# First mixer of a two-layer hybrid backbone: the product of probabilities and values as unsplit fp32 matmuls of 64 output rows each, and the place of the spread of the softmax denominators

## The reference

```python
def softmax_with_sink(s, sink):
    s_all = jnp.concatenate([s, jnp.broadcast_to(sink, s.shape[:-1] + (1,))], axis=-1)
    return jax.nn.softmax(s_all, axis=-1)[..., :-1]

def attend(q, k, v, ok, sink, scale):
    s = jnp.einsum('bqhgd,bkhd->bhgqk', q, k).astype(jnp.float32) * scale
    if ok is not None:
        s = jnp.where(ok, s, NEG_INF)
    p = softmax_with_sink(s, sink[None, :, :, None, None])
    return jnp.einsum('bhgqk,bkhd->bqhgd', p.astype(v.dtype), v)

# latent queries see a window of latent keys and all context keys; context queries see context keys
bx = conformer_conv(px[..., i_u:], w_dw, b_dw, ln_g, ln_b)   # GLU, 31 taps, layer norm, SiLU
ox = jnp.concatenate([ax, bx], axis=-1) @ w_out
```

## Time and profile before

| | |
|---|---|
| median of 3 runs | 1679.69 us |
| profiled execution | 1684.07 us, its span 1682.2 us |
| PE busy | 1649.3 us, 98% |
| DVE busy | 1132.4 us, 67% |
| ACT busy | 603.7 us, 36% |
| POOL busy | 126.2 us, 8% |
| first mixer's attention loop | from 446 us to 573 us of the span |

### The profile page before, as it was taken

The page is one execution under the profiler, slowest core; times in us unless marked ns, Lnnn a source line. Parts: engine busy times, 40 slices in busy tenths (PEclk is TensorE's granted clock), DMA queues, the critical chain, the costliest instruction groups (busy, mean ns, idle before and its releaser), DMA issues.

```text
span 1682.2 us, 23652 instructions
## 1 busy us (share of the span) xinstructions
PE 1649.3 (98%) x8871; PEld 1414.0 (84%) x8871; DVE 1132.4 (67%) x1885; ACT 603.7 (36%) x817; POOL 126.2 (8%) x81
## 2 busy tenths in 40 slices
PE   8999999999999899999999999999999999999998
PEld 6788888889877698888888898888888888989997
DVE  5878777777585678787787873463333687666665
ACT  3321222223776532212212342212222356444443
POOL 0000000000796100000000000000000011000000
PEclk7999999999999999999999999999999999999999
DMA  7754554542211035555555323342222231155552
GB/s 296 281 202 181 194 198 187 204 150 97 101 51 50 26 133 189 191 189 210 190 197 191 139 75 121 149 149 84 104 88 100 101 105 72 50 183 197 184 198 75
DMA packets 45426, 247.45 MB, mean 147 GB/s; under 512 B 5168, under 2 KB 5296, under 8 KB 25008
## 3 DMA queue, kind: packets, MB, share of 16 engines
q1 hardware_dynamic: 45360, 246.55, 40.2%
HBM read 245.48 MB, written 1.05 MB: 147 GB/s over the span
## 4 chain that ended last, share of the span: by engine, by line
PE 89%; DVE 5%; POOL 2%; issue 2%; ACT 1%; DMA 0%; SPq 0%; ACTq 0%; POOLq 0%; DVEq 0%
PE ps L1828 13%; PE ps L1830 13%; PE ps L1837 13%; PE ps L1659 10%; PE ps L1661 10%; PE ps L1660 10%; PE ps L2303 5%; PE ps L1686 4%; PE ps L2309 2%; POOL spare L571 2%; PE ps L1945 1%; PE ps L1866 1%; PE ps L2026 1%; DVE w_lo L1221 1%; PE ps L1900 1%
## 5 line engine op out<-in xcount | busy, mean ns | idle before, releaser
L1828 PE MATMUL ps<-a_hi,w_hi 128*128 128x512 f32 x960 | 373.8, 389 | 0.8 <-ACT w_hi L687 0.8
L1830 PE MATMUL ps<-a_lo,w_hi 128*128 128x512 f32 x960 | 373.5, 389 | 0.0
L1221 DVE TENSOR_TENSOR w_lo<-raw,w_hi 128x2048 fp32r<-128x2048 f32 x114 | 260.5, 2288 | 49.3 <-ACT w_hi L687 21.7
L1659 PE MATMUL ps<-h_hi,w_lo 128*128 128x512 f32 (+1 forms) x648 | 234.9, 362 | 1.5 <-POOL h_lo L577 1.4
L1661 PE MATMUL ps<-h_hi,w_hi 128*128 128x512 f32 (+1 forms) x648 | 233.4, 360 | 0.0
L1660 PE MATMUL ps<-h_lo,w_hi 128*128 128x512 f32 (+1 forms) x648 | 233.4, 360 | 0.0
L1837 PE MATMUL ps<-a_hi,w_lo 128*128 128x512 f32 x960 | 227.3, 389 | 0.0
L1828 PEld LDWEIGHTS ps<-a_hi,w_hi 128*128 128x128 f32 x960 | 180.2, 188 | 38.9 <-issue 0.8
L1837 PEld LDWEIGHTS ps<-a_hi,w_lo 128*128 128x128 f32 x960 | 180.2, 188 | 37.4
L1830 PEld LDWEIGHTS ps<-a_lo,w_hi 128*128 128x128 f32 x960 | 180.2, 188 | 37.3
L681 ACT ACTIVATE work<-ps 128x512 f32<-128x512 f32 x66 | 39.5, 599 | 431.2 <-PE ps L1837 418.7
(11 more groups left out here) (344 smaller groups left out, 2525.7 us busy)
## 6 DMA issues: line engine op xcount, KB each, us to landing
raw<-wstream SPq DMA_DIRECT2D x147, 1024.0 KB, 4.9
mring<-wmod SPq DMA_DIRECT2D x144, 512.0 KB, 3.5
spare<-wstream SPq DMA_DIRECT2D x11, 1024.0 KB, 4.8
xT<-tokens SPq DMA_DIRECT2D x4, 512.0 KB, 5.1
cb<-cond SPq DMA_DIRECT2D x1, 1024.0 KB, 8.0
out<-mring SPq DMA_DIRECT2D x4, 256.0 KB, 2.1
mring<-gain SPq DMA_DIRECT2D x1, 512.0 KB, 6.5
cst<-consts SPq DMA_DIRECT2D x1, 449.0 KB, 7.0
```

Of the source, the lines that this page charges most:

```text
L1221: dve.tensor_tensor(w_lo[:, slot], raw[:, slot], w_hi[:, slot].bitcast(F32), ALU.subtract).then_inc(lo_ready, 1)
L1659: pe.matmul(dst, lhs_lo, rhs_hi, start=start, stop=False, skip_group_check=True)
L1828: pe.matmul(bank, hi, a_hi[:, k, 0:nt], start=k == 0, stop=False, skip_group_check=True)
L1830: pe.matmul(bank, hi, a_lo[:, k, 0:nt], start=False, stop=False, skip_group_check=True)
```

## The change

The turned probabilities are kept once, as fp32 (`ab_pt`), and the lo half, DVE's 24 subtractions, is gone. The values, turned once on PE as before, are kept as fp32 too (`ab_v`), so their hi and lo halves are gone. The outputs of a pair become fp32 matmuls of 64 columns of stationary values: for each block of 128 keys one for unit u = 0 into rows 0 to 63 and one for u = 1 into rows 64 to 127 of the same bank columns, 8 matmuls of 128 columns or 4 of 256 for a pair. The pair's result is therefore one 128-row block, and DVE scales it with one instruction instead of two. The spread lies in the bank's second half and moves: at odd i PE does outputs of pair (i-5)/2 and directly behind them the spread of pair (i-3)/2, so the first spread is at i = 3. On ACT the copy of the spread moves from the front of step i to behind exp and the copy of the turned probabilities, and waits for the scaling of the last pair. PE's transposes wait for ACT's copy instead of DVE's subtraction. The query tiles keep their steps and get new numbers, since tile 5 has left the list.

```diff
-            ab_pt_hi = sb("ab_pt_hi", [P, 2, 2, TOK], F32R, where=turned)
-            ab_pt_lo = sb("ab_pt_lo", [P, 2, 2, TOK], F32R, where=turned)
+            ab_pt = sb("ab_pt", [P, 2, 2, TOK], where=turned)
+            ab_v = sb("ab_v", [P, TOK], where=turned)
...
-        AB_PT = [(x[:, 0], x[:, 1]) for x in (ab_pt_hi, ab_pt_lo)]
+        AB_PT = (ab_pt[:, 0], ab_pt[:, 1])
...
-            act.wait_ge(slab_done, w + 2)
+            act.wait_ge(step_done, 1)
+            act.activation(ab_v[:], ps[1][:], ACT.Copy).then_inc(v_turned, 1)
             ab_high(1)
+            split_hi(G1, G1 % 2, G1)
             ab_high(2)
-            split_hi(G1, G1 % 2, G1)
-            ab_high(3)
             glu_tanh(0)
             act.wait_ge(slab_done, G0 + 1)
             split_hi(G2, G2 % 2, G2)
...
-                if i >= 5 and i % 2 and (i - 5) // 2 < AB_PAIRS:
-                    p = (i - 5) // 2
-                    n = P * len(units[2 * p][1])
-                    r0 = spread_at(p)
-                    act.wait_ge(spread_done, p + 1)
-                    if p >= 2:
-                        act.wait_ge(o_scaled, p - 1)
-                    act.activation(rspread[:, p % 2, 0:n], ps[AB_O_BANK][:, r0:r0 + n], ACT.Copy).then_inc(spread_copy, 1)
...
-                    act.activation(pt_unit(AB_PT[0], e, units[e][1]), pt_bank(e, units[e][1]),
+                    act.activation(pt_unit(AB_PT, e, units[e][1]), pt_bank(e, units[e][1]),
                                    ACT.Copy).then_inc(pt_hi, 1)
+                if i >= 5 and i % 2 and (i - 5) // 2 < AB_PAIRS:
+                    p = (i - 5) // 2
+                    n = P * len(units[2 * p][1])
+                    act.wait_ge(spread_done, p + 1)
+                    if p >= 1:
+                        act.wait_ge(o_scaled, p)
+                    act.activation(rspread[:, p % 2, 0:n], ps[AB_O_BANK][:, LAT:LAT + n], ACT.Copy).then_inc(spread_copy, 1)
...
+            ab_turn(1)
+            ab_low(1)
             ab_turn(2)
-            ab_low(1)
+            glu(0)
             ab_low(2)
-            ab_turn(3)
-            glu(0)
-            ab_low(3)
...
-                if 3 <= i < len(units) + 3:
-                    e = i - 3
-                    qts = units[e][1]
-                    dve.wait_ge(pt_hi, e + 1)
-                    dve.tensor_tensor(pt_unit(AB_PT[1], e, qts), pt_bank(e, qts),
-                                      pt_unit(AB_PT[0], e, qts).bitcast(F32), ALU.subtract).then_inc(pt_lo, 1)
...
+                    dve.wait_ge(spread_copy, p + 1)
                     dve.wait_ge(pv_done, p + 1)
-                    dve.wait_ge(spread_copy, p + 1)
+                    dve.wait_ge(spread_done, min(p + 2, AB_PAIRS))
                     if p >= 2:
                         dve.wait_ge(ot_lo, p - 1)
-                    for u in range(2):
-                        rows = slice(A_DIM * u, A_DIM * (u + 1))
-                        last = dve.tensor_tensor(onorm[rows, p % 2, 0:n], ps[AB_O_BANK][rows, u * n:(u + 1) * n],
-                                                 rspread[rows, p % 2, 0:n], ALU.mult)
-                    last.then_inc(o_scaled, 1)
+                    dve.tensor_tensor(onorm[:, p % 2, 0:n], ps[AB_O_BANK][:, 0:n], rspread[:, p % 2, 0:n],
+                                      ALU.mult).then_inc(o_scaled, 1)
...
+            def unit_outputs(p):
+
+                qts = units[2 * p][1]
+                n = len(qts) * P
+                turned_pair = AB_PT[p % 2].rearrange("p a n -> p (a n)")
+                tiles = TOK // n
+                for k in range(tiles):
+                    for u in range(2):
+                        v, c = qts[0][1] + k * P + A_DIM * u, (2 * k + u) * n
+                        last = pe.matmul(ps[AB_O_BANK][A_DIM * u:A_DIM * (u + 1), 0:n], ab_v[:, v:v + A_DIM],
+                                         turned_pair[:, c:c + n], start=k == 0, stop=k == tiles - 1,
+                                         skip_group_check=True)
+                last.then_inc(pv_done, 1)
+
+            def unit_spreads(p):
+
+                for b in range(len(units[2 * p][1])):
+                    c = LAT + b * P
+                    for u in range(2):
+                        col = units[2 * p + u][2][b]
+                        last = pe.matmul(ps[AB_O_BANK][A_DIM * u:A_DIM * (u + 1), c:c + P],
+                                         rinv[:, col:col + 1].to_broadcast([P, A_DIM]), ident,
+                                         start=True, stop=True, skip_group_check=True)
+                last.then_inc(spread_done, 1)
+
             EARLY = {21: (0, (0, 1)), 23: (1, (0,)), 25: (1, (1,)), 27: (2, (0, 1))}
-            units = AB_UNITS
             for i in range(len(units) + 4):
                 if i < len(units):
                     h, qts, _ = units[i]
                     if i == 0:
                         pe.wait_ge(key_zeros, 2)
-                        pe.wait_ge(piece_lo, 3)
+                        pe.wait_ge(piece_lo, 2)
+                        pe.wait_ge(v_turned, 1)
                     if i in (6, 12, 18):
-                        pe.wait_ge(piece_lo, 3 + i // 6)
...
-                        pe.wait_ge(pt_lo, e - 1)
+                        pe.wait_ge(pt_hi, e - 1)
...
-                if i >= 5 and i % 2:
-                    p = (i - 5) // 2
-                    pe.wait_ge(rinv_ready, p + 1)
-                    if p >= 1:
-                        pe.wait_ge(o_scaled, p)
...
-                    last.then_inc(spread_done, 1)
                 projections(2 * i + 1)
...
                 if i >= 5 and i % 2:
-                    p = (i - 5) // 2
-                    qts = units[2 * p][1]
-                    n = len(qts) * P
-                    pe.wait_ge(pt_lo, 2 * p + 2)
-                    pe.wait_ge(spread_copy, p + 1)
-                    tiles = TOK // n
-                    for k in range(tiles):
-                        at = [x[p % 2].rearrange("p a n -> p (a n)")[:, 2 * k * n:2 * (k + 1) * n] for x in AB_PT]
-                        v = (qts[0][1] // P + k) * P
-                        last = passes(ps[AB_O_BANK][:, 0:2 * n], h_hi[:, 5, v:v + P], h_lo[:, 5, v:v + P], *at,
-                                      k == 0, k == tiles - 1)
-                    last.then_inc(pv_done, 1)
+                    pe.wait_ge(pt_hi, i - 3)
+                    pe.wait_ge(spread_copy, (i - 5) // 2 + 1)
+                    unit_outputs((i - 5) // 2)
+                if i >= 3 and i % 2 and (i - 3) // 2 < AB_PAIRS:
+                    pe.wait_ge(rinv_ready, (i - 3) // 2 + 1)
+                    unit_spreads((i - 3) // 2)
```

More of the change, by code:

```diff
@@ L288, in build @@
         v_copy = sem("v_copy")
+        v_turned = sem("v_turned")
         ot_hi = sem("ot_hi")
@@ L356, in one_part @@
             return [(slice(0, P), hi[:, i])], [(slice(0, P), hi[:, i], lo[:, i])]
-        AB_LOWS = (((LOW, h_hi[LOW, 4], keys_lo[LOW, 0]), (HIGH, h_lo[HIGH, 4], keys_lo[HIGH, 1])), None)
+        AB_LOWS = (((LOW, h_hi[LOW, 4], keys_lo[LOW, 0]), (HIGH, h_lo[HIGH, 4], keys_lo[HIGH, 1])),)
         AB_LOWS += tuple(((LOW, h_hi[LOW, t], h_hi[HIGH, t]), (HIGH, h_lo[HIGH, t], h_lo[LOW, t])) for t in range(4))
-        AB_PIECES = [(0, 4, (slab_done, W_AB + 1), True), (1, 5, (step_done, 1), False)]
-        AB_PIECES += [(2 + t, t, (slab_done, W_AB + 2), True) for t in range(2)]
-        AB_PIECES += [(4, 2, (step_done, 2), True), (4, 3, (slab_done, Q23 + 1), True)]
+        AB_PIECES = [(0, 4, (slab_done, W_AB + 1))]
+        AB_PIECES += [(2 + t, t, (slab_done, W_AB + 2)) for t in range(2)]
+        AB_PIECES += [(4, 2, (step_done, 2)), (4, 3, (slab_done, Q23 + 1))]
         N_AB = len(AB_PIECES)
-        AB_TURN = (1, None, 2, 3, 4, 5)
         MLA_STEPS = [(("kr", 0),), (("q", 0), ("q", 1)), (("q", 2), ("q", 3)), (("q", 4), ("q", 5))]
@@ L792, in ab_high @@
             def ab_high(j):
[L794 to L801, removed]
+                bank, tile, _ = AB_PIECES[j]
+                act.wait_ge(turned_done, j + 1)
                 act.activation(h_hi[LOW, tile], ps[bank][LOW], ACT.Copy)
@@ L878, in _ @@
                 if i == 11:
-                    act.wait_ge(step_done, 2)
-                    ab_high(4)
+                    ab_high(3)
                 if i == 14:
@@ L886, in _ @@
                     split_hi(W_AB + 9, (W_AB + 9) % 2, W_AB + 9)
-                    ab_high(5)
+                    ab_high(4)
                 if i == 20:
@@ L1324, in ab_turn @@
             def ab_turn(j):
-                bank, _, (s, value), _ = AB_PIECES[j]
+                bank, _, (s, value) = AB_PIECES[j]
                 dve.wait_ge(s, value)
-                n = AB_TURN[j] - 1
-                src, t1 = ps[bank][:, 0:LAT], sq[:, n // 2 % 2, half(n % 2)]
+                src, t1 = ps[bank][:, 0:LAT], sq[:, j // 2 % 2, half(j % 2)]
                 link(dve.tensor_tensor(t1, src, cos, ALU.mult))
@@ L1335, in ab_low @@
             def ab_low(j):
```

(23 more changed lines are left out.)

19 lines of the change are left out of this document (9 added, 10 removed).

## The result

| | before | after |
|---|---|---|
| median of 20 runs each | 1679.72 us (1678.42 to 1682.24) | 1682.77 us (1681.34 to 1687.54) |
| profiled execution (span) | 1684.07 us (1682.2) | 1685.19 us (1683.3) |
| PE, DVE busy | 1649.3, 1132.4 us | 1643.9, 1114.4 us |

What follows compares the result with a forecast made beforehand. PE, busy 98% of the span, was taken as the bound. Loop terms reached −2.3, with clock −0.3 in all: 1684.07 − 0.3 = 1683.8 profiled, 1679.4 us median after the carried 4.4; range 1672.0 to 1685.0.

Steps and rivals of the forecast that it cites:

- The tail, steps 20 to 27: Loop's last steps up to the attention tile: 28.1 us from step 20's scores, before 26.87; −2.3 in all, before clock.
- the 4.4 us between the profile and the median: Profiled execution's excess over the timed median before the change, carried over to turn 1683.8 into 1679.4 us.
- PE's own work: PE's spreads and outputs in the loop: 24.2 us before, 18.1 after, so 6.1 less.
- The fixed 0.31 for each block: Cost on PE of entering and leaving the 64-row form, 0.31 us for each of 13 blocks.
- Steps 3 to 19: Loop up to step 20's scores: cumulative +1.3 at step 6, −1.6 at 12, −3.5 at 16, still −3.5 at 20.
- The half clock behind step 5 and behind the query tile: Slow-clock costs after PE's waits at steps 5 and 12: 0.7 us and 0.85 us.
- The −1.6 of step 12: Scores of step 12 at 501.15, 1.6 us earlier in all, with 1.5 of the 1.76 wait left.
- In the tail, where chains cover part: Clock term for the waits at steps 21 and 23: 1.3 us, partly covered by chains.
- new waits and half clock: Slower rival: five low-clock stretches instead of two, each 1.7 us; +3.4 against before, 1683.1 us; chance 0.15.
- The copy that is never late: Faster rival: PE never waits late for ACT's copy of the spread; about −7.3, 1672.4 us; chance 0.28.
- Missing overlap: Slower rival: array halves do not overlap on different operands; 10.6 more on PE, +8.0 against before, 1687.7 us; chance 0.10.
- the 3.4 us that were to be told from no change: Whole-kernel measurement threshold, about 0.2%: what a measurement can tell from no change.

Runs made afterwards that it cites:

- filler: Changed kernel plus 12, 10 and 13 unused matmuls of 512 columns on PE at steps 17, 21 and 23, inside its waits for the copy: 1680.73 us, ratio 0.9999.

## Why the prediction was wrong

The forecast was 0.3 us less than before; measured are 3.05 more. The mechanism that it named, a late copy and half clock behind its waits, is the one that acted. Two terms failed. The tail, steps 20 to 27, was sized 2.0 us too short, for chains that were to cover the half clock. And the 4.4 us between the profile and the median were carried over as if they were the kernel's, which cost another 1.9. A body of the loop that came out 1.1 better than the sum hid part of it. By its own steps:

- **PE's own work** was right in kind, and too cautious in one term. 0.055 a record held, and the halves overlap with different operands. The fixed 0.31 for each block was mis-sized: outputs and spread of steps 5 and 15 take 1.24 and 1.23 (518.80 to 520.03), where the sum had 1.41, and step 7's 1.46, where it had 1.63. So PE saved about 8 us and not 6.1. The Trainium skill (TensorEngine Tiling (Array Packing), Key Properties) has the drain at a change of mode; the runs put it at 0.14 (1.24 less 20 × 0.055) to 0.31 here.
- **Steps 3 to 19** came out right, with some luck. With 0.46 taken off, by which this execution entered the loop later, the scores of steps 6, 12, 16 and 20 start at 471.80, 501.27, 519.57 and 542.67, forecast 471.75, 501.15, 520.3 and 543.05. The waits came as forecast in place and size: 2.19 (2.0), 1.26 (1.5), 3.70 (3.9). The half clock behind step 5 and behind the query tile, counted with 0.7 and 0.85, did not come in this execution; steps 16 to 19 took 0.35 longer than forecast. The −1.6 of step 12 is not what its terms give: a tile 1 us sooner means 501.7, and the listed wins of the blocks bring PE there at 500.9, where 1.5 of waiting asks for 499.65. Measured, the tile came 1.44 sooner and PE 0.94. A wait of before that the sum left out is gone:

```profile
485.94 1.62 PE L2011 MATMUL ps<-a_hi,w_hi 128*128 128x512 f32 x6 [0.77 <-ACT w_hi L612]
```

- **Steps 20 to 27** failed by 2.0: the chain was up to 1.0 too short, the clock in it 1.0 too small. In times from step 20's scores:

| | forecast | without low clock (filler) | changed kernel |
|---|---|---|---|
| outputs of step 21 | 8.25 | 8.49 | 8.49 |
| outputs of step 23 | 16.65 | 17.26 | 18.64 |
| outputs of step 25 | 21.25 | 22.19 | 24.45 |
| attention tile | 28.1 | 29.14 | 31.40 |

  The forecast added 1.3 for the clock; measured are 2.26 (31.40 − 29.14) for two stretches. The chain is at most 1.0 longer than forecast, part of it the filler's overrun at step 23, where PE no longer waits. "In the tail, where chains cover part" is the clause that failed: each slow stretch lay on the outputs, the scores and the transposes for which DVE and ACT were waiting, so it was part of the chain, not under its cover. (Which operations these were is read from the timeline; that the stretches cost time is shown by the filler.)
- **From the profile to the median.** Profile against profile the change is +1.1 us: 0.7 in the loop, 0.5 ahead of it, where nothing was changed. So the sign was lost in the tail already. The other 1.9 is the carried distance: the forecast took it that a profiled execution lies 4.4 above the median; after, it lies 2.4 above. The other profiles of before show that the 4.4 were that execution's own: one stretch more in the loop than either of the two, one more behind the loop than one of them, and the latest start of the loop of the three. The changed kernel's profile is a common one: 9 of its 20 executions took 1684.5 us or more. Against the two other profiles of before, the body of the loop wins 2.4 and not 3.9, and the tail loses 4.5: +2.1. The rest of the 3.05, about 0.9, stays open. The mean granted clock of the changed kernel's runs goes down to 0.987, its profiles are at 0.988 and 0.990, and those of before at 0.990 to 0.994; more stretches in the loop would fit, but so would some elsewhere, and none of these executions was profiled.
- **The rivals.** The slower one, new waits and half clock, gave 1683.1 with a chance of 0.15; the time was 1682.77. That the number fits is in part luck. It had five stretches instead of two, at 1.7 each; the profiles have three in the loop where before has one or two, at 1.1 to 1.6 each, and the rest of the loss is the longer chain. The copy that is never late gave 1672.4: not this change, but with the copy moved to the front and ahead of the squares 1672.94. There too the agreement is partly luck, since PE's own work saved more than that rival had and 5.0 us of waits for the copy were left. Missing overlap is refuted by the 0.055. And the 3.4 us that were to be told from no change were too many: the interval is 1.1 us to either side.

The Trainium skill (TensorE: Matmul & The Clock Gate, Part 1) has the throttled state as the default that activity lifts; the kernel with filler agrees, with no stretch where the changed kernel has three. By that rule the slower rival could have had more of the chance.

## What to carry to other kernels

When a producer is moved on a queue, follow its consumer: a copy of 0.3 us placed behind two operations of its step cost 7 us, and each move to the front gave its part back. Take two or three profiles of the same kernel before a sum is built on its low-clock stretches, since the waits repeat to 0.01 us and the stretches do not, and see where the profiled execution lies among the timed ones before its distance to the median is carried over. And expect a shortened engine to arrive early at the next wait: ask for each saved microsecond what delivers the work behind it.

## What the runs showed of the hardware

- The same wait brings a stretch of half clock in one execution and not in another: behind 1.76 in two of three profiles of the kernel before, behind 2.82 in two of three, behind the 1.57 near the end in two of three. Behind the 2.2 of step 5 it came in two of five profiles of kernels that have this wait. Behind the changed kernel's waits of 3.1 to 3.7 it came in every profile of it, six of six. In the loop a stretch costs 1.1 to 1.6 us (2.26 for the two of the tail, 1.56 for that of step 17, 1.5 and 1.6 in the kernel before).
- fp32 matmuls of 64 rows run beside those of the other half even when several of the same half stand before them in the program, and a record that stands later in the program can start before one that stands earlier: spreads of the lower half at 481.67, outputs of the upper half at 481.77. A pair's outputs and spread take 1.95 instead of 1.46, where no overlap would add 0.9.
